# The gate-only work of the mLSTM moved into the input projection: 32 partitions of (head, chunk) in place of 4 partitions of heads

## What is computed

```python
b = jnp.cumsum(lf_c, axis=-1)                      # lf = log_sigmoid(forget gate), within the chunk
log_d = jnp.where(causal, b[..., :, None] - b[..., None, :] + i_c[..., None, :], -jnp.inf)
log_inter = b + m_prev[..., None]
m = jnp.maximum(log_inter, jnp.max(log_d, axis=-1))
w_intra = jnp.exp(log_d - m[..., None])
w_inter = jnp.exp(log_inter - m)
...
h = num / jnp.maximum(jnp.abs(den), jnp.exp(-m))[..., None]
m_next = jnp.maximum(b_last + m_prev, jnp.max(log_w_state, axis=-1))
decay = jnp.exp(b_last + m_prev - m_next)
w_state = jnp.exp(log_w_state - m_next[..., None])
```

## Time and profile before

| | |
|---|---|
| median of 3 runs | 2331.73 us (2330.88 to 2335.7) |
| the profiled execution | 2334.58 us |
| its span | 2332.8 us |
| TensorE (PE) busy | 2165.6 us, 93% |
| VectorE (DVE) busy | 1628.8 us, 70% |
| ScalarE (ACT) busy | 1214.0 us, 52% |
| mean granted clock of TensorE | 0.961 of full |

### The profile page before, as it was taken

How to read it: one execution, slowest core, us unless ns; L and a number is a source line. 1 busy time by engine, 2 the same in 40 slices (tenths; PEclk the granted TensorE clock), 3 DMA queues, 4 the chain that set the end, 5 groups by cost and what they waited for, 6 DMA issues and landing times. The chain is left out here.

```text
span 2332.8 us, 32427 instructions
## 1 busy us (share of the span) xinstructions
PE 2165.6 (93%) x10466; PEld 1800.8 (77%) x10467; DVE 1628.8 (70%) x1862; ACT 1214.0 (52%) x1241; POOL 558.7 (24%) x539
## 2 busy tenths in 40 slices
PE   6999876889589999999999999999999999999993
PEld 5787876668378888888888888888888888888872
DVE  4688756646775665768678785778875787686774
ACT  4422233233164554657467574766755576565653
POOL 1001221102520111305125131522511252121401
PEclk9999967999589999999999999999999999999997
DMA  6123261541395676869779886988996798687974
GB/s 177 55 82 140 79 126 45 171 167 55 132 380 206 229 233 197 292 233 358 264 269 371 306 287 216 316 305 280 365 318 197 251 367 311 227 278 263 314 233 179
DMA packets 285812, 540.81 MB, mean 232 GB/s; under 512 B 37154, under 2 KB 53586, under 8 KB 284658
## 3 DMA queue, kind: packets, MB, share of 16 engines
q1 hardware_dynamic: 260306, 490.51, 59.9%
q0 software_dynamic: 25440, 49.47, 8.2%
HBM read 513.06 MB, written 64.57 MB: 248 GB/s over the span
## 5 line engine op out<-in xcount | busy, mean ns | idle before, releaser
L2402 DVE TENSOR_TENSOR ex_w_lo<-ex_raw,ex_w_hi 128x2048 fp32r<-128x2048 f32 x408 | 926.7, 2289 | 373.2 <-ACT ex_w_hi L2295 306.5
L2295 ACT CAST ex_w_hi<-ex_raw 128x2048 fp32r<-128x2048 f32 x371 | 706.7, 1911 | 278.8 <-PE ex_ps_g L2611 99.8
L2206 POOL TENSOR_TENSOR ex_passed<-ex_ident 128x1 f32<-128x1 f32 x136 | 134.0, 985 | 1183.6 <-ACT ex_y L2338 1152.6
L2610 PE MATMUL ex_ps_g<-ex_w_hi,ex_x_hi 128*128 128x512 f32 x784 | 307.4, 392 | 8.4 <-issue 6.5
L2610 PE MATMUL ex_ps_l<-ex_w_hi,ex_x_hi 128*128 128x512 f32 x784 | 308.8, 394 | 1.2 <-DVE ex_w_lo L2402 1.2
L2611 PE MATMUL ex_ps_g<-ex_w_lo,ex_x_hi 128*128 128x512 f32 x784 | 305.5, 390 | 0.0
L2611 PE MATMUL ex_ps_l<-ex_w_lo,ex_x_hi 128*128 128x512 f32 x784 | 305.3, 389 | 0.0
L2610 PE MATMUL ex_ps_y<-ex_w_hi,ex_h_hi 128*128 128x512 f32 x544 | 217.1, 399 | 0.6
L2614 PE MATMUL ex_ps_g<-ex_w_hi,ex_x_lo 128*128 128x512 f32 x544 | 212.3, 390 | 0.0
L2614 PE MATMUL ex_ps_l<-ex_w_hi,ex_x_lo 128*128 128x512 f32 x544 | 212.0, 390 | 0.0
L2611 PE MATMUL ex_ps_y<-ex_w_lo,ex_h_hi 128*128 128x512 f32 x544 | 211.9, 390 | 0.0
(11 more groups left out here) (464 smaller groups left out, 3746.9 us busy)
## 6 DMA issues: line engine op xcount, KB each, us to landing
ex_raw<-in_w_up_dram SPq DMA_DIRECT2D x272, 1024.0 KB, 8.7
ex_raw<-in_w_down_dram SPq DMA_DIRECT2D x136, 1024.0 KB, 8.1
st_tab<-tabs SPq DMA_DIRECT2D x8, 1408.0 KB, 7.3
pr_raw<-in_w_in_dram SPq DMA_DIRECT2D x10, 1024.0 KB, 5.4
tabs<-pr_x POOLq DMA_DIRECT2D x32, 256.0 KB, 2.3
por_raw<-in_w_out_dram SPq DMA_DIRECT2D x16, 256.0 KB, 4.7
t<-mix_sig_o SPq DMA_DIRECT2D x8, 512.0 KB, 2.6
fi_h<-h SPq DMA_DIRECT2D x8, 512.0 KB, 7.6
```

The source lines that it names most:

```text
L2206: pool.tensor_tensor(passed[:, :], ident[:, 0:1], ident[:, 0:1], ALU.add).then_inc(passed_done, 1)
L2295: nc.scalar.copy(w_hi[:, j % SPLIT, :, :], raw[:, j % RAW, :, :]).then_inc(hi_done, 1)
L2402: v.tensor_tensor(w_lo[:, j % SPLIT, :, :], raw[:, j % RAW, :, :], w_hi[:, j % SPLIT, :, :].bitcast(F32), ALU.subtract).then_inc(lo_done, 1)
L2610: pe.matmul(to[:, :], hi_in[:, b, kk, :], w_hi[:, s, k, :], start=first, stop=False)
```

## The change

All that depends on the gates alone is made in `project`. The gates go to a new DRAM tensor (L317 of the changed kernel, two DMAs) and come back as `gate_rows`, 32 partitions (head h, chunk c) by 2 by 128 tokens (L331, two DMAs), in the half of `raw` that no weight piece uses any more. ACT makes the log there, now after unit 33 instead of 40. DVE makes the running sum and maximum of each chunk by itself (`rows_within`). PE turns the 32 chunk ends into one row on one partition; DVE joins them with one short scan for each head (`over_chunks`), PE spreads the result, and DVE finishes the rows (`rows_across`). Five tiles of columns `cols`, the rows `m_rows` and the identity are kept for `mlstm`, which loses its constants, its rows, its transposes and its copies. `spread_m` picks a row with one column of the identity, spread over 128 columns, in place of `sel`: 32 partitions are contracted instead of 4. The zeroing of `st["toep"]` on POOL now stands behind the first `query`.

```diff
-        "gates": sb("gates", [HEADS, 2, T], F32),
+        "ident": sb("ident", [P, P], F32),
+        "m_rows": sb("m_rows", [HEADS * NC, CH], F32),
+        "cols": sb("cols", [P, 5, HEADS * NC], F32),
...
-        LOG_AT = 40
+        LOG_AT, ENDS_AT, CARRY_AT, COLS_AT = 33, 36, 38, 40
...
                 for n in range(PRAW, len(pieces)):
+                    if n == len(pieces) - 1:
+                        sp.wait_ge(unit_read, read_count("gates", 0, 1))
+                        for g in range(2):
+                            sp.dma_start(gates_dram[g], gates[:, g, :]).then_inc(gates_out, 16)
...
+                sp.wait_ge(gates_out, 32)
+                sp.wait_ge(lo_done, len(pieces) - 1)
+                for g in range(2):
+                    sp.dma_start(gate_rows[:, g, :], gates_dram[g].rearrange("h (c t) -> (h c) t", c=NC)).then_inc(gates_in, 16)
...
+                pool.wait_ge(lo_done, len(pieces) - 1)
+                pool.memset(zeros, 0.0).then_inc(row_consts, 1)
+                pool.memset(ones, 1.0).then_inc(row_consts, 1)
+                pool.memset(carried, 0.0).then_inc(row_consts, 1)
                 pool.wait_ge(rho_set, 1)
...
                     if m == LOG_AT:
-                        act.wait_ge(lo_done, len(pieces))
-                        act.wait_ge(unit_read, read_count("gates", 0, 1))
-                        nc.scalar.activation(f_abs, mix["gates"][:, 1, :], ACT.Abs).then_inc(abs_set, 1)
+                        act.wait_ge(gates_in, 32)
+                        nc.scalar.activation(f_abs, gate_rows[:, 1, :], ACT.Abs).then_inc(abs_set, 1)
...
+                    if m == ENDS_AT:
+                        act.wait_ge(ends_turned, 1)
+                        nc.scalar.copy(chunk_ends, ps_c[0:1, 0:2 * HC].rearrange("p (r k) -> p r k", r=2)).then_inc(ends_copied, 1)
+                    if m == CARRY_AT:
+                        act.wait_ge(carried_spread, 1)
+                        nc.scalar.copy(m_in[:, :], ps_c[0:HC, 4 * HC:4 * HC + 1]).then_inc(m_in_set, 1)
+                        nc.scalar.copy(cols[:, 3, :], ps_c[:, 2 * HC:3 * HC]).then_inc(cols_set, 1)
+                        nc.scalar.activation(cols[:, 4, :], ps_c[:, 3 * HC:4 * HC], ACT.Exp).then_inc(cols_set, 1)
+                    if m == COLS_AT:
+                        act.wait_ge(cols_ready, 1)
...
+                    if m == ENDS_AT:
+                        pe.wait_ge(loc_set, 1)
+                        pe.transpose(ps_c[0:1, 0:HC], m_rows[:, CH - 1:CH], ident[0:HC, 0:HC])
+                        pe.transpose(ps_c[0:1, HC:2 * HC], log_sum[:, CH - 1:CH], ident[0:HC, 0:HC]).then_inc(ends_turned, 1)
+                    if m == CARRY_AT:
+                        pe.wait_ge(carried_set, 1)
...
+                    if m == COLS_AT:
+                        pe.wait_ge(rows_set, 1)
+                        pe.wait_ge(cols_set, 2)
+                        for r in range(3):
+                            mm = pe.transpose(ps_c[:, (5 + r) * HC:(6 + r) * HC], b_rows[:, r, :], ident[0:HC, 0:HC])
+                        mm.then_inc(cols_ready, 1)
...
+                def rows_within():
+                    gate_f = gate_rows[:, 1, :]
+                    v.wait_ge(gates_in, 32)
+                    v.wait_ge(log_set, 1)
+                    v.wait_ge(row_consts, 3)
+                    link(v.scalar_tensor_tensor(gate_f, gate_f, 0.0, f_abs, ALU.min, ALU.subtract))
+                    link(v.tensor_tensor_scan(log_sum, zeros, gate_f, 0.0, ALU.add, ALU.add))
+                    link(v.tensor_tensor(b_rows[:, 0, :], gate_rows[:, 0, :], log_sum, ALU.subtract))
+                    v.tensor_tensor_scan(m_rows[:, :], zeros, b_rows[:, 0, :], -3.0e38, ALU.add, ALU.max).then_inc(loc_set, 1)
+
+                def over_chunks():
+                    v.wait_ge(ends_copied, 1)
+                    for h in range(HEADS):
+                        own = slice(h * NC, h * NC + NC - 1)
+                        ins = v.tensor_tensor_scan(carried[:, 0, h * NC + 1:(h + 1) * NC], chunk_ends[:, 0, own], chunk_ends[:, 1, own],
+                                                   0.0, ALU.max, ALU.add)
...
+                def rows_across():
+                    v.wait_ge(m_in_set, 1)
...
+                rows_within()
                 for q in range(QUADS):
                     turn_tables(q)
-                gate_f = mix["gates"][:, 1, :]
-                v.wait_ge(log_set, 1)
-                v.scalar_tensor_tensor(gate_f, gate_f, 0.0, f_abs, ALU.min, ALU.subtract).then_inc(log_f_set, 1)
-                v.wait_ge(log_f_set, 1)
-
+                    if q == 2:
+                        over_chunks()
+                    if q == 5:
+                        rows_across()
...
                 query(0)
+                pool.memset(st["toep"][:, :, :], 0.0).then_inc(st["zeroed"], 1)
...
-                        mm = pe.matmul(by_head(ps_m)[:, h, :], sel[:, h, :], M[:, steps(c)], start=True, stop=True)
+                        at = h * NC + c
+                        mm = pe.matmul(by_head(ps_m)[:, h, :], ident[0:HC, at:at + 1].to_broadcast([HC, P]), m_rows[:, :],
+                                       start=True, stop=True)
...
+                v.wait_ge(consts_set, 3)
                 mask_m(0)
-                v.wait_ge(cols_set, 5)
                 v.wait_ge(small_in, 16)
```

More of the change, by code:

```diff
@@ L140, in project @@
         neg_half = sb("neg_half", [P, 1], F32)
-        ident = sb("ident", [P, P], F32)
+        ident = mix["ident"]
+        gates = sb("gates", [HEADS, 2, T], F32)
+        HC = HEADS * NC
+        m_in = sb("m_in", [HC, 1], F32)
         h_hi = sb("h_hi", [P, KD, T], F32R)
@@ L398, in read @@
                         for g in range(2):
-                            ins = nc.scalar.activation(mix["gates"][:, g, part * 512:(part + 1) * 512],
+                            ins = nc.scalar.activation(gates[:, g, part * 512:(part + 1) * 512],
                                                        bank[32 * g:32 * g + HEADS, :], ACT.Identity, bias=b_gates[:, g:g + 1])
@@ L467, in _ @@
                         nc.scalar.activation(f_abs, f_abs, ACT.Ln, bias=1.0).then_inc(log_set, 1)
+                    if m == ENDS_AT:
[8 more added lines that the diff above has]
+                        act.wait_ge(cols_ready, 1)
+                        nc.scalar.copy(cols[:, 0, :], ps_c[:, 5 * HC:6 * HC]).then_inc(cols_set, 1)
+                        nc.scalar.activation(cols[:, 1, :], ps_c[:, 6 * HC:7 * HC], ACT.Exp).then_inc(cols_set, 1)
+                        nc.scalar.activation(cols[:, 2, :], ps_c[:, 7 * HC:8 * HC], ACT.Exp, scale=-1.0).then_inc(cols_set, 1)
             @block.tensor
@@ L865, in mlstm, with col @@
         out = sb("out", [P, NC, HEADS, HD + 1], F32)
-        early = out[:, :, :, :].rearrange("p c h e -> p (c h e)")
-        not_first = early[0:HEADS, 2 * T:3 * T]
-        carry = early[0:HEADS, 3 * T:4 * T]
-        b = sb("b", [HEADS, T], F32)
-        M = sb("M", [HEADS, T], F32)
-        rows = sb("rows", [HEADS, 3, T], F32)
-        ends = sb("ends", [HEADS, 2, NC], F32)
-        sel = sb("sel", [HEADS, HEADS, P], F32)
-        ident = sb("ident", [P, P], F32)
+        ident, m_rows = mix["ident"], mix["m_rows"]
         mask = sb("mask", [P, P], F32)
+        HC = HEADS * NC
+        def col(i):
+            return mix["cols"][:, i, :].rearrange("p (h c) -> p h c", h=HEADS)
+        a_col, w_state, exp_neg_m, m_before, decay = (col(i) for i in range(5))
         neg_half = sb("neg_half", [P, 2, HEADS], F32)
         norm_g = sb("norm_g", [P, HEADS], F32)
-        a_col = sb("a_col", [P, NC, HEADS], F32)
-        w_state = sb("w_state", [P, NC, HEADS], F32)
-        exp_neg_m = sb("exp_neg_m", [P, NC, HEADS], F32)
-        m_before = sb("m_before", [P, HEADS, NC], F32)
-        decay = sb("decay", [P, HEADS, NC], F32)
         masked = sb("masked", [P, HEADS, CH], F32)
@@ L975, in power @@
                     pool.tensor_tensor(rstd[:, batch, :], var_h[:, batch, :], neg_half[:, 0:batch.stop - batch.start, :], ALU.pow).then_inc(pow_done, 1)
-                pool.memset(st["toep"][:, :, :], 0.0).then_inc(st["zeroed"], 1)
                 def query(c):
@@ L1011, in weights @@
                     for h in range(HEADS):
-                        ins = nc.scalar.activation(weight[:, h, :], masked[:, h, :], ACT.Exp, bias=a_col[:, c, h:h + 1])
+                        ins = nc.scalar.activation(weight[:, h, :], masked[:, h, :], ACT.Exp, bias=a_col[:, h, c:c + 1])
                     ins.then_inc(weight_done, 1)
@@ L1049, in _ @@
             def _(pe):
-                pe.wait_ge(consts_set, 11)
-                pe.wait_ge(rows_set, 1)
-                for r in range(3):
-                    for c in range(NC):
-                        at = (r * NC + c) * HEADS
-                        pe.transpose(ps_t[:, at:at + HEADS], rows[:, r, steps(c)], ident[0:HEADS, 0:HEADS])
-                for h in range(HEADS):
```

(6 more changed lines are left out.)

73 lines of the change are left out of this document (31 added, 42 removed).

## The result

The changed kernel took 2318.91 us in the median (2317.12 to 2320.97), against 2332.46 for the kernel before on the same chip: a ratio of 0.9941, with an interval of 0.9925 to 0.9957. It is faster by 13.6 us (0.6%), where 18.0 were forecast; the forecast of 2313.7 and its range up to 2318.5 were too low. The profiled execution took 2317.68 us, 16.9 less than that of before; 2316.6 were forecast for it.

The account below looks back on a forecast made before the run. PE, busy 2165.6 of 2332.8 us, was taken to bound the kernel, so only its wait between `project` and `mlstm` could give much. Start 17.4 us earlier plus 0.6 on the first spread: 2331.73 - 18.0 = 2313.7 us, range 2308.5 to 2318.5.

Parts of the forecast that it names:

- The rule of the Trainium skill: ACT's log ahead of `hi(10)`: 2.66 us per table switch, DVE late by 1.1 us, time 2314.8; 3 in 100.
- the thirteen small operations: DVE's added row work in `project`: seven of 0.34 us and six of 0.16, 3.4 us, between 2.1 and 4.4.
- The rival of the gates' way through DRAM: In `project`, gates' reads land late, ACT waits ahead of `hi(10)`; slower, 2341 if they take 40 us; 3 in 100.
- The broadcast spread over 32 partitions: PE's spread in `mlstm` with a repeated weight column: no added cost taken, at most 0.9 us for each of 8.
- 285.8 + 2.05 = 287.85: End of `project` at its last store's landing plus the boundary; `spread_m(0)` there instead of 305.31, -17.4 us.
- my own signs for being right: Included `spread_m(0)` within 2.2 us of `project`'s last landing, PE idle under 4 us, rest of `mlstm` unchanged within 3 us.
- the 0.6 us: First spread in `mlstm` at full clock, 1.15 us instead of 2.05; 0.6 of the 0.9 us counted.
- My rival of the clock: PE's clock stays up at the start of `mlstm`, saving 3.5 us (2310.8) or up to 7.3 (2307.0); 14 in 100.
- The rival of a dear start: Late second query after zeroing, `project` ending at 286.9 or slow broadcast weights give back 1 to 4 us, up to 2317.7; 15 in 100.

Follow-up runs that it names:

- the marks: Changed kernel plus three tiny memsets: two on POOL (behind its last store issue and its last wait), one on DVE behind that store's landing; 2317.0 us, one execution.
- SP's stores: Kernel before, with the 16 turn-table stores issued from SP instead of POOL; ratio 1.0008 (0.9996 to 1.0021).
- more on DVE: Changed kernel with three more 128x512 operations (about 2.1 us) on DVE ahead of the last turn tables; 2321.49 us, ratio 0.9955.

## Why the prediction was off

**Right.** The gate rows left the path whole: `spread_m(0)` starts with its stage, and no engine waits for a piece of the new work. The log: two loads of 1.28 us and three activations of 0.3; `hi(10)` ran from 240.82 to 242.71, forecast 241.0 to 242.9. The rule of the Trainium skill (ScalarE: Activation LUTs, "What ACT_TABLE_LOAD costs") that a drain adds 1.38 us to a switch is not what this trace shows: the exponential starts 0.01 us behind its table load. DVE was idle nowhere, and the thirteen small operations took 3.1 us, forecast 3.4; the last table came at 284.04, as 1.3 us were lost ahead of them already (`lo(10)` at 245.88). The rival of the gates' way through DRAM fell: nobody waited for that load. The broadcast spread over 32 partitions costs what the one over 4 did, 2.04 for eight at half clock. PE ended at 285.33, forecast 285.0, and ACT at 285.96.

**The step that failed: "285.8 + 2.05 = 287.85".** I took the boundary to cost 2.05 us behind the stage's last landing, from one place where I took DVE to end last. POOL's drain stands between the two. With the landing at 286.7 (284.33 and the 2.35 of the marks) the stage began 5.6 us behind it. The stage's end has two branches: about 1.2 us behind the last computing engine's end (1.16 to 1.18 us in five runs), and 1.0 to 1.2 us behind the end of POOL's drain, which for a late store is some 7.9 us behind its issue. Before, the two lay close together: 280.06 + 7.86 = 287.92, against 285.89 + 1.2 = 287.1. What the change adds to DVE was therefore not hidden behind ACT, as I had it, but moved POOL's last issue by 4.27 us (280.06 to 284.33), and the stage's start with it (287.92 to 292.29, 4.37 us). With this in the sum, the forecast would have been 2313.7 + 4.4 = 2318.1. The sign stood in rows that I had read: POOL idle for 7.32 us ahead of its first constant. I didn't ask why. Of my own signs for being right, three failed: the spread within 2.2 us of the last landing, PE idle for under 4 us at the boundary, and the rest of `mlstm` unchanged within 3 us (it was 4.1 shorter). The idle time stands a second time in each kernel, at the start of the last stage, here in the changed one behind an indirect DMA:

```profile
2281.30 1.55 POOL L2262 DMA_INDIRECT h<-ex_y,ex_nowhere  x1 [0.30 <-issue]
2290.46 0.10 POOL L2731 MEMSET fi_neg_half<- 128x1 f32 x1 [7.61 <-POOLq L86]
```

**The clock.** In the profiled execution two errors nearly cancelled. The first spread came 4.5 us later than forecast (292.33 against 287.85), and what follows it up to S5 was 3.5 us shorter than forecast (4.1 us less, where 0.6 were counted). That 2317.68 came so close to 2316.6 is luck. The pause was 7.0 us and not 2.9, so the first spread ran at half clock (2.04, forecast 1.15): the 0.6 us were not won. Against that the clock was at half for only 6.7 us of the stage, against 14.5 behind the first spread before, though the wait for `norm_g` cost 1.48 us. Whether the 4.1 us belong to the change is open. The stretch took 84.03 us before and 84.00 before with SP's stores; with the change and POOL's late stores it took 79.93, 80.17 (marks) and 79.19 (more on DVE), but 83.61 in the same changed kernel on another chip. The start alone is 12.98 us, near the 13.55 of the medians, which can't separate the two. My rival of the clock had the size right (3.5 to 7 us) but not the condition: the clock did not stay up, and a short pause at the boundary doesn't surely buy it either.

The rival of a dear start came near in its total, 2317.7, but not in its mechanism: the zeroing of `toep` ran at 298.71 and kept nobody waiting.

## What to carry to other kernels

Ask of each stage boundary which engine is released last and what it does behind its last instruction; look for the drains on the line that opens the block, POOL's above all. Price a boundary by the branch that will decide after the change, not by its cost before. Work that is put on an idle engine isn't hidden if another queue's last issue hangs on it. Where a stage ends with stores, give them to SP, or see that POOL's last is early: 7.9 less 1.2 gives some 7 us ahead of the last engine's end, an estimate; 11.3 us was enough (274.55 against 285.81). With one wait put where its data is read this was worth 0.33 to 0.4% more (0.9908 against 0.9941, and 0.9916 against 0.9956 on one chip), more than half of what the change itself brought. With four stores from SP in place of sixteen it was 0.9928, not clear of the 0.9941.

## What the runs showed of the hardware

- The next stage began 7.9 to 8.0 us behind POOL's last issue of a 256 KB store in eight traces (7.85 to 7.98) in which nothing else decided; the store itself was seen as landed after 2.35 us. Behind a load of 4 bytes it was 6.2 us. Stores issued by SP left only 1.2 us behind the last engine.
- Most of that is a drain of POOL at the end of its block: 3.99 to 4.18 us where it had stored 31 or 32 tables, 3.75 with 28, 2.77 with 16, whether its last DMA was just over or 50 us old. What the drain waits for the traces don't show.
- With pauses of 3.7 to 8.2 us at the boundary PE ran at half clock for the first 4.6 to 14 us of the next stage, in six executions of versions of the changed kernel; the longest pause did not go with the longest time at half (8.23 us with 4.6, 5.79 with 14). With a pause of 1.83 us the clock was still full at the start of the stage in five; it then fell, for 3.4 us in four of them and for 10.2 us in the fifth.
- Where PE was kept busy across a pause the stretch behind it was 2.8 to 6 us shorter; of the three totals one was 2.5 us lower and two were no better. Where the rest goes is open.
